# Projections moved between the small compression steps of a fused transformer kernel, and its last expert finished in quarters

## The chip, the cores and the metric

The kernel runs on one core of a Trainium2 chip. The metric is device time in microseconds (us) of one execution. Engines are written as in the profile: PE is TensorE (PEld its weight loads), DVE is VectorE, ACT is ScalarE, POOL is GpSimd, SP is SyncE, which here only issues DMAs. PE's clock has two levels, 1.2 and 2.4 GHz; the profile gives the granted clock as a share of the higher one.

## The reference

A batch of one, 256 tokens, width 1024. Two layers of a first block are followed by one hybrid layer. Everything is float32.

```python
for l in range(2):
    mod = silu(c) @ w_ada[l] + b_ada[l]           # nine shifts, scales, gates
    x = x + 0.5 * g1 * swiglu(modulate(x, sh1, sc1), ...)
    x = x + g2 * token_mix(modulate(x, sh2, sc2), ...)
    x = x + 0.5 * g3 * swiglu(modulate(x, sh3, sc3), ...)
x = rms_norm(x) * final_norm
# hybrid layer: convolution and forgetting attention, then
out = 0
for e in range(32):                               # each token has two experts of one group of 8
    out = out + comb[..., e:e+1] * ((silu(h @ w_gate[e]) * (h @ w_up[e])) @ w_down[e])
return x + gate2 * out
```

The part of `token_mix` that the change reorders:

```python
k_c = gelu(blocks(kc) @ cmpk_w1) @ cmpk_w2        # 15 compressed keys per group; v_c likewise
p_c = masked_softmax(q_a @ k_c.T * scale - slope * d_c); o_c = p_c @ v_c
q = (rms_norm(cq) * mla_q_norm) @ mla_w_uq        # 8 heads x (64 + 32), rope on the last 32
ckv = rms_norm(ckv) * mla_kv_norm
k_nope = ckv @ mla_w_uk;  v = ckv @ mla_w_uv
```

## The kernel before

Each engine has one program, written out by hand, and the engines meet at semaphores. Nothing is scheduled by a tool: the order of the lines in an engine's program is the order of its work.

**Weights.** All weights stream from HBM in units of three blocks of 128 x 2048 floats (1 MB each). SP loads a block into `raw` once the block before it in that place has been split. A split is two halves of 128 x 1024: ACT rounds a half to `w_hi` (L504, for the experts L512), DVE subtracts to get `w_lo` (L933, for the experts L940). ACT may write a place of `w_hi` only when PE has released it (`used[j]`). Every product of an activation with a weight is three matmuls (`mm3`, L1717 to L1719: high by high, high by low, low by high), so 128 x 512 outputs over 128 rows of depth cost three 512-column matmuls.

**The stretch in the token mix** (program of PE from L2016, of DVE from L1319, of ACT from L690). PE turns the latents cq and ckv, q, the selected and window keys, and the keys and values to be compressed (`bank[2]`, `bank[3]`, L2025). Then:

- 16 `keep_warm` matmuls with a matrix of zeros (L1707), while DVE copies the turned rows and builds `blocks` (L1324, L1325, L1331);
- 16 matmuls that compress (L2036), gelu on ACT (L700), 12 small ones that make compressed keys and values (L2044, L2047), 8 more zero matmuls, 16 small score matmuls (L2057);
- q's up-projection: four banks, 36 matmuls of 384 columns; meanwhile DVE and ACT run the softmax of the compressed scores;
- 4 transposes of p (L2073), k's up-projection (12 matmuls of 512), the 16 products with compressed values (L2086), v's up-projection (12 of 512);
- 32 transposes of q and k heads (L1968), and the attention jobs begin: scores of job 0 (L1920), scores of job 1 after DVE has added job 0's bias, and the merge gates' matmuls between jobs (L1717).

DVE applies rope after ACT has copied q's up-projection (L708), copies k's and v's out (L1381, L1396), scales the compressed output (L1390) and copies turned k (L1400). Blocks 1 and 2 of unit `u_mix + 3` are split after all up-projections of q.

```python
                keep_warm(16, SPARE[:, 64:512])
                pe.wait_ge(blocks_ready, l + 1)
                pe.wait_ge(cqT_ready, l * 3 + 3)
                carry_waits()
```

**The experts.** Tokens are gathered into four tiles of 128 by group, and the 32 experts run one after the other on a group's tile: 24 matmuls of gate and up, 12 of down, where expert e's down follows e+1's gate and up. A group's output y stands in `ACC[0]` and `ACC[1]`; `sparse_out` splits it (ACT L880, DVE L1673), and `spread` (L2315) distributes the rows to token order in the four SPREAD banks, summed over the groups. After the last group `x_update` multiplies each SPREAD bank with `gate_bc` into `upd` (L1032) and adds it to x (L1035), token tile by token tile, and SP writes x with one DMA (L464). The last expert's down weights go into place 2 of `w_hi`, which PE releases when expert 30's down is done.

## Time and profile before

| | us |
|---|---|
| median of 3 runs | 1877.88 (1874.67 to 1884.23) |
| the profiled execution's own time | 1885.67 |
| its span in the profile | 1884.0 |
| PE busy | 1785.5 (95%) |
| DVE busy | 1373.1 (73%) |
| ACT busy | 957.4 (51%) |
| POOL busy | 47.0 (2%) |
| mean granted TensorE clock | 0.97 |
| read from HBM | 435.36 MB, 232 GB/s over the span |

Busy shares are means over stages with different limits, and PE counts as busy on zero matmuls and at half clock too. In a timeline row the first number is the start in us from the span's start, the second the length of the merged piece; matmuls overlap, so what one costs is the distance between two starts. A count on PE's rows of float32 products that are not split counts two records for each matmul.

### The profile page before, as it was taken

How to read it: one execution, taken by the hardware profiler on the slowest of the kernel's cores; microseconds unless marked ns; L12 is line 12 of the kernel's file. 1: busy time of each engine (PE TensorE's matmuls, PEld its weight loads, DVE VectorE, ACT ScalarE, POOL GpSimd, SP SyncE). 2: the span in 40 equal slices, each digit the busy share in tenths (PEclk: the TensorE clock that was granted, in tenths of full speed). 3: DMA queues.
4: the chain of work that ended last, by engine and by line, in shares of the span. 5: the costliest groups of instructions: out<-in, count | busy, mean ns of one | idle time of the engine just before them, and what ended most of it. 6: DMA issues, size and time to landing. Idle time of an engine off the chain costs nothing.

```text
span 1884.0 us, 24972 instructions
## 1 busy us (share of the span) xinstructions
PE 1785.5 (95%) x8677; PEld 1443.0 (77%) x8693; DVE 1373.1 (73%) x2091; ACT 957.4 (51%) x1433; POOL 47.0 (2%) x92
## 2 busy tenths in 40 slices
PE   5999999999999999999999999999899897999996
PEld 3788787877788878887878777887787766888875
DVE  6878675856876578777657678776776477998985
ACT  3444453664544454444436554444444546777773
POOL 0000000000000000000000000000000000000000
PEclk8999998999999999999979999999899998999998
DMA  8988651234576658884513348986563433999992
GB/s 366 362 333 302 255 203 63 93 120 170 202 288 245 247 216 322 310 325 174 191 48 110 118 150 298 350 304 231 188 246 108 183 134 138 375 350 363 359 346 98
DMA packets 61499, 437.45 MB, mean 232 GB/s; under 512 B 6768, under 2 KB 7280, under 8 KB 9200
## 3 DMA queue, kind: packets, MB, share of 16 engines
q1 hardware_dynamic: 47200, 339.27, 48.1%
q0 software_dynamic: 12672, 92.28, 13.2%
q10 hardware_dynamic: 1552, 4.89, 0.7%
q8 instruction: 48, 0.79, 0.2%
q14 instruction: 27, 0.22, 0.0%
HBM read 435.36 MB, written 1.05 MB: 232 GB/s over the span
## 4 chain that ended last, share of the span: by engine, by line
PE 83%; DVE 11%; ACT 4%; issue 1%; DMA 1%; ACTq 0%; SPq 0%; DVEq 0%; POOLq 0%
PE bank L1717 24%; PE bank L1718 24%; PE bank L1719 24%; DVE w_lo L933 3%; PE bank L1940 2%; DVE ada_w L957 1%; ACT w_hi L504 1%; PE bank L1958 1%; PE bank L1799 1%; DMA ada_w<-ada_pairs 1%; PE bank L1920 1%; PE bank L1707 1%; DVE arena L1032 1%; DVE w_lo L940 1%; DVE arena L1232 1%
## 5 line engine op out<-in xcount | busy, mean ns | idle before, releaser
L933 DVE TENSOR_TENSOR w_lo<-raw,w_hi 128x1024 fp32r<-128x1024 f32 x426 | 501.5, 1220 | 223.5 <-ACT w_hi L504 222.9
L504 ACT ACTIVATE w_hi<-raw 128x1024 fp32r<-128x1024 f32 x426 | 426.2, 1052 | 363.5 <-PE bank L1719 359.6
L1717 PE MATMUL bank<-w_hi,uT_hi 128*128 128x512 f32 (+3 forms) x1424 | 558.4, 392 | 19.5 <-DVE uT_lo L1251 11.9
L1718 PE MATMUL bank<-w_lo,uT_hi 128*128 128x512 f32 (+3 forms) x1424 | 544.2, 382 | 0.0
L1719 PE MATMUL bank<-w_hi,uT_lo 128*128 128x512 f32 (+3 forms) x1424 | 543.7, 382 | 0.0
L1717 PEld LDWEIGHTS bank<-w_hi,uT_hi 128*128 128x128 f32 x1424 | 271.6, 191 | 78.7 <-DVE uT_lo L1251 12.9
L1719 PEld LDWEIGHTS bank<-w_hi,uT_lo 128*128 128x128 f32 x1424 | 270.9, 190 | 52.1
L1717 PE MATMUL bank<-w_hi,r_arena 128*128 128x512 f32 (+1 forms) x744 | 301.9, 406 | 8.1 <-DVE r_arena L1634 4.9
L1718 PEld LDWEIGHTS bank<-w_lo,uT_hi 128*128 128x128 f32 x1424 | 271.5, 191 | 48.7 <-issue 1.4
L1718 PE MATMUL bank<-w_lo,r_arena 128*128 128x512 f32 (+1 forms) x744 | 298.6, 401 | 0.0
L1719 PE MATMUL bank<-w_hi,r_arena 128*128 128x512 f32 (+1 forms) x744 | 295.7, 397 | 0.0
L957 DVE CUSTOM_DVE_ANT_0 ada_w<-ada_w,cmpw 128x1024 f32<-128x1024 f32 x176 | 206.9, 1218 | 6.3 <-DMA ada_w<-ada_pairs 6.3
L1717 PEld LDWEIGHTS bank<-w_hi,r_arena 128*128 128x128 f32 x744 | 143.0, 192 | 43.7 <-DVE r_arena L1634 5.6
L1719 PEld LDWEIGHTS bank<-w_hi,r_arena 128*128 128x128 f32 x744 | 142.8, 192 | 33.3
L1718 PEld LDWEIGHTS bank<-w_lo,r_arena 128*128 128x128 f32 x744 | 142.9, 192 | 30.6
L940 DVE TENSOR_TENSOR w_lo<-raw,w_hi 128x1024 fp32r<-128x1024 f32 x96 | 113.2, 1221 | 13.1 <-ACT w_hi L512 13.1
L512 ACT ACTIVATE w_hi<-raw 128x1024 fp32r<-128x1024 f32 x96 | 96.2, 1053 | 17.7 <-PE bank L1719 17.7
L554 ACT ACTIVATE arena<-bank 128x256 f32<-128x256 f32 x88 | 33.8, 386 | 121.9 <-PE bank L1719 121.9
L940 DVE TENSOR_TENSOR w_lo<-ada_w,w_hi 128x1024 fp32r<-128x1024 f32 x64 | 75.3, 1221 | 9.7 <-ACT w_hi L512 8.9
L474 POOL DMA_DIRECT2D ada_w<-ada_pairs x88 | 46.8, 531 | 1342.1 <-DVE mods_gate L957 594.6
L512 ACT ACTIVATE w_hi<-ada_w 128x1024 fp32r<-128x1024 f32 x64 | 64.1, 1054 | 13.6 <-PE bank L1719 13.6
L1707 PE MATMUL bank<-zeros 128*128 128x512 bf16 (+1 forms) x236 | 57.7, 399 | 6.3 <-DMA cst<-shape_constants 5.8
(324 smaller groups left out, 1474.8 us busy)
## 6 DMA issues: line engine op xcount, KB each, us to landing
raw<-weight_stream SPq DMA_DIRECT2D x216, 1024.0 KB, 4.9
ada_w<-ada_pairs POOLq DMA_DIRECT2D x88, 1024.0 KB, 5.2
raw<-expert_blocks SPq DMA_DIRECT2D x48, 1024.0 KB, 4.9
ada_w<-expert_blocks SPq DMA_DIRECT2D x32, 1024.0 KB, 4.8
cmpw<-expert_blocks SPq DMA_DIRECT2D x16, 1024.0 KB, 4.9
arena<-ada_pairs SPq DMA_DIRECT2D x5, 1024.0 KB, 13.9
ada_w<-ada_pairs SPq DMA_DIRECT2D x3, 1024.0 KB, 13.3
cmpw<-compress_w ACTq DMA_DIRECT2D x2, 1024.0 KB, 8.1
```

The lines of the kernel that those rows point to most:

```text
L474: pool.dma_start(ada_w[:, slot], ada[g]).then_inc(ada_landed[slot], 16)
L504: act.activation(w_hi[:, b], v, ACT.Copy).then_inc(hi_done, 1)
L512: act.activation(w_hi[:, b], v, ACT.Copy).then_inc(hi_done, 1)
L554: act.activation(act_g[:, t], GU[t][:, 0:F_UNIT], ACT.Silu).then_inc(silu_done, 1)
L933: V.tensor_tensor(w_lo[:, b], v, f32(w_hi[:, b]), ALU.subtract).then_inc(split_done, 1)
L940: V.tensor_tensor(w_lo[:, b], v, f32(w_hi[:, b]), ALU.subtract).then_inc(split_done, 1)
L957: e = V.tensor_tensor_reduce(w[:, i], w[:, i], c, 1.0, 0.0, ALU.mult, ALU.add, dst[:, i:i + 1])
L1707: pe.matmul(dst, zeros[:, 0:P], zeros[:, 0:dst.shape[1]], start=True, stop=True, skip_group_check=True)
L1717: pe.matmul(dst, xh, w_hi[:, off:off + n], start=first, stop=False, skip_group_check=True)
L1718: pe.matmul(dst, xh, w_lo[:, off:off + n], start=False, stop=False, skip_group_check=True)
L1719: return pe.matmul(dst, xl, w_hi[:, off:off + n], start=False, stop=last, skip_group_check=True)
L1940: m = pe.matmul(HT[:, a * DH:(a + 1) * DH], pT[j % 2][:, kt, a], v, start=kt == 0, stop=kt == qt, skip_group_check=True)
```

## The change

Nothing is computed differently, save that the gate of the expert layer multiplies each group's output before it is spread, instead of the sum after.

In the token mix PE's order becomes: q's up-projection right behind the turns of the keys and values to be compressed, in place of the 16 zero matmuls; compression; k's up-projection of token tile 0; the small matmuls of compressed keys and values; k's of tile 1 and v's of tile 0, in place of the 8 zero matmuls; compressed scores; v's of tile 1; transposes of p; q's turns; products with compressed values; k's turns. Banks are dealt out anew for this. DVE builds k's rope part while it has no other work, applies q's rope before compression is done, and takes the copies and splits between.

At the end, the last expert's down weights go to place 0 of `w_hi` (free after its own first four k steps), the down product runs output half by output half, each half is gated (`y_gated`), split, spread, added to x in quarters of 128 x 512, and each quarter has its own DMA.

The core of the diff (not shown: new bank numbers in copies, `first_mod` folded into `mod_ready`, which shifts counts by 3, and the same edits in the branch for a group of over 128 tokens, which this input does not enter):

PE, token mix:

```diff
                 m.then_inc(c_psum, 1)
-                keep_warm(16, SPARE[:, 64:512])
+                pe.wait_ge(q_ready, l * 2 + 2)
+                pe.wait_ge(ks_ready, l + 1)
+                pe.wait_ge(kw_ready, l + 1)
+                seen = set()
+                for b in range(4):
+                    for k in range(3):
+                        off = UQ_OFF + k * 768 + (b % 2) * 384
+                        need(u_mix + 2, seen, off, 384)
+                        m = mm3(bank[UQ_BANKS[b]][:, 0:384], cqT_hi[:, k, tok(b // 2)], cqT_lo[:, k, tok(b // 2)], off, 384, k == 0, k == 2)
+                    m.then_inc(uq_psum, 1)
+                for j in (1, 2):
+                    release(used[j])
...
+
+                def up(t, b, off, done):
+                    for k in range(2):
+                        m = mm3(b[:, :], cqT_hi[:, 3 + k, tok(t)], cqT_lo[:, 3 + k, tok(t)], off + k * 512, 512, k == 0, k == 1)
+                    m.then_inc(done, 1)
+
+                need(u_mix + 3, set(), 0, BLK)
+                up(0, bank[2], 0, uk_psum)
                 pe.wait_ge(hidc_ready, l + 1)
-                pe.wait_ge(q_ready, l * 2 + 2)
+                pe.wait_ge(uq_copied, l * 4 + 4)
                 carry_waits()
...
-
-                keep_warm(8, SPARE[:, 64:512])
+                up(1, bank[3], 0, uk_psum)
+                up(0, bank[0], 1024, uv_psum)
                 pe.wait_ge(kvc_ready, l + 1)
...
+                up(1, bank[1], 1024, uv_psum)
+                release(used[0])
...
+
+                pe.wait_ge(rope_done, l + 1)
+                pe.wait_ge(uk_copied, l * 2 + 2)
+                pe.wait_ge(uv_ready, l * 2 + 2)
+                for b in range(4):
+                    if b == 2:
+                        pe.wait_ge(cp_ready, l + 1)
+                    for i in range(2):
+                        m = turn_rows(bank[Q_BANKS[b]][:, i * S:i * S + S], lambda t, h: q_tok[:, t, h], 2 * b + i, QK)
+                    m.then_inc(qm_psum, 1)
...
                 for b in range(4):
+                    if b < 2:
+                        pe.wait_ge(qm_ready, l * 4 + 3 + b)
+                    else:
+                        pe.wait_ge(co_done, l + 1)
                     for i in range(2):
                         m = turn_rows(bank[K_BANKS[b]][:, i * S:i * S + S], lambda t, h: k_tok[:, t, h], 2 * b + i, QK)
                     m.then_inc(km_psum, 1)
```

ACT and DVE, token mix:

```diff
+                for b in range(4):
+                    act.wait_ge(uq_psum, l * 4 + b + 1)
+                    act.activation(q_tok[:, b // 2, 4 * (b % 2):4 * (b % 2) + 4].rearrange("p h c -> p (h c)"), bank[UQ_BANKS[b]][:, 0:384],
+                                   ACT.Copy).then_inc(uq_copied, 1)
+                split(u_mix + 3, (1,))
                 act.wait_ge(hidc_psum, l + 1)
                 act.activation(hid_cmp[:, :, :, 0:N_CMP], bank[4][:, 0:64].rearrange("p (k g n) -> p k g n", k=2, g=GROUPS)[:, :, :, 0:N_CMP],
                                ACT.Gelu_apprx_tanh).then_inc(hidc_ready, 1)
+                split(u_mix + 3, (2,))
...
+                dve.wait_ge(uq_copied, l * 4 + 4)
+                dve.wait_ge(blocks_ready, l + 1)
+                qr = q_tok[:, :, :, NOPE:QK]
...
+
+                def up_k(t):
+                    dve.wait_ge(uk_psum, l * 2 + t + 1)
+                    V.tensor_copy(k_tok[:, t, :, 0:NOPE], bank[2 + t][:, :].rearrange("p (h c) -> p h c", h=HEADS)).then_inc(uk_copied, 1)
+
+                def up_v(t):
+                    dve.wait_ge(uv_psum, l * 2 + t + 1)
+                    V.tensor_copy(vm[:, t], bank[t][:, :]).then_inc(uv_ready, 1)
+
+                up_k(0)
...
                 e.then_inc(kvc_ready, 1)
-
                 link(V.memset(p_cmp[:, :, :], 0.0))
+                up_k(1)
+                up_v(0)
+                split(u_mix + 3, (2,))
...
+                up_v(1)
```

The expert end (ACT, DVE, PE, SP):

```diff
+                place, sem_, count = expert_place(half, odd, 2, IN_LINE)
+                act.wait_ge(sem_, count)
+                act.wait_ge(used[0], half * 2 + (MOE_U0 + odd + 2))
+                for b, v in halves(0, place):
+                    act.activation(w_hi[:, b], v, ACT.Copy).then_inc(hi_done, 1)
+
...
-                act.wait_ge(ys_psum, n + 1)
                 for h in range(2):
-                    act.activation(y_hi[:, h * 512:(h + 1) * 512], ACC[h][:, :], ACT.Copy).then_inc(ys_hi_done, 1)
+                    act.wait_ge(ys_gated, 2 * n + h + 1)
+                    act.activation(y_hi[:, h * 512:(h + 1) * 512], y_gated[:, h * 512:(h + 1) * 512], ACT.Copy).then_inc(ys_hi_done, 1)
...
+                for h in range(2):
+                    dve.wait_ge(ys_psum, 2 * n + h + 1)
+                    V.tensor_tensor(y_gated[:, h * 512:(h + 1) * 512], ACC[h][:, :], gate_bc[:, h * 512:(h + 1) * 512], ALU.mult).then_inc(ys_gated, 1)
...
+            def last_update(n):
+                for i, (h, t) in enumerate([(h, t) for h in range(2) for t in range(T)]):
+                    dve.wait_ge(spread_done, 4 * n + i + 1)
+                    xt = x[:, t, h * 512:(h + 1) * 512]
+                    V.tensor_tensor(xt, xt, SPREAD[2 * t + h][:, :], ALU.add).then_inc(x_ready, 1)
...
-            x_update(n6 + 1, (spread_done, 1), SPREAD)
+            last_update(0)
...
+                for h in range(2):
+                    for c in range(2):
+                        m = mm3(ACC[h][:, :], hTs_hi[:, c], hTs_lo[:, c], at_ + c * D + h * 512, 512, False, done and c == 1)
+                    if done and h == 0:
+                        m.then_inc(ys_psum, 1)
...
-                        if last and h == 1:
-                            m.then_inc(first_tile if t == 0 else spread_done, 1)
+                        if last:
+                            m.then_inc(spread_done, 1)
...
-            sp.dma_start(out.rearrange("(t p) d -> p t d", p=P), x[:, :, :]).then_inc(out_landed, 16)
+            for i, (h, t) in enumerate([(h, t) for h in range(2) for t in range(T)]):
+                sp.wait_ge(x_ready, 2 * (3 * DEPTH + 3) + i + 1)
+                sp.dma_start(out[t * P:(t + 1) * P, h * 512:(h + 1) * 512], x[:, t, h * 512:(h + 1) * 512]).then_inc(out_landed, 16)
+            sp.wait_ge(out_landed, 64)
```

**On PE, token mix, from the turns of compressed keys on.** L2025 are those turns, L1707 the zero matmuls, L1702 carries waits, L2036 compression, L2044 and L2047 make the compressed keys and values, L2057 scores. Before:

```order
L2025 MATMUL bank<-cst,arena 64x128 x15
L1707 MATMUL bank<-zeros 128x448 x16
L1702 MATMUL bank<-zeros 128x1 [waits cqT_ready,blocks_ready]
L2036 MATMUL bank<-arena,cmpw 128x4x15 x16
L1702 MATMUL bank<-zeros 128x1 [waits q_ready,hidc_ready]
L2044 MATMUL bank<-arena,lvec 64x15 x2
L2047 MATMUL bank<-lvec,arena 15x64 x4
L2044 MATMUL bank<-arena,lvec 64x15 x2
L2047 MATMUL bank<-lvec,arena 15x64 x4
L1707 MATMUL bank<-zeros 128x448 x8
L2057 MATMUL bank<-arena 128x15 [waits kvc_ready]
L2057 MATMUL bank<-arena 128x15 x15
L1717 MATMUL bank<-w_hi,r_arena 128x384 [waits blocks_split,kw_ready,ks_ready]
```

With the change (L1754 to L1756 are `mm3`; the 36 rows of q's up-projection stand above these):

```order
L1735 MATMUL bank<-zeros 128x1 x2
L1739 MATMUL bank<-zeros 128x1 [waits cqT_ready,blocks_ready]
L2084 MATMUL bank<-arena,cmpw 128x4x15 x16
L1754 MATMUL bank<-w_hi,r_arena 128x512 [waits blocks_split]
L1755 MATMUL bank<-w_lo,r_arena 128x512
L1756 MATMUL bank<-w_hi,r_arena 128x512
L1754 MATMUL bank<-w_hi,r_arena 128x512
L1755 MATMUL bank<-w_lo,r_arena 128x512
L1756 MATMUL bank<-w_hi,r_arena 128x512
L1739 MATMUL bank<-zeros 128x1 [waits uq_copied,hidc_ready]
L2100 MATMUL bank<-arena,lvec 64x15 x2
L2103 MATMUL bank<-lvec,arena 15x64 x4
```

The zero matmuls are gone, q's 36 matmuls fill the time in which DVE builds the blocks, and six matmuls of k's stand between compression and what needs its gelu.

**On ACT, token mix.** L695 and L697 copy q, L698 and L700 the selected keys. Before, the two activation functions stand first, then q's up-projection is copied out (L708), then p (L711), then both splits (L504):

```order
L698 ACTIVATE arena<-bank 128x512 [waits ks_psum]
L700 ACT_TABLE_LOAD
L700 ACTIVATE arena<-bank 128x4x15 [waits hidc_psum]
L704 ACT_TABLE_LOAD
L704 ACTIVATE arena<-arena 128x16x15 [waits cs_ready]
L708 ACTIVATE arena<-bank 128x384 [waits uq_psum] x4
L711 ACTIVATE arena<-bank 128x512 [waits cp_psum]
L504 ACTIVATE w_hi<-raw 128x1024 [waits block_used1,block_landed1]
L504 ACTIVATE w_hi<-raw 128x1024
L504 ACTIVATE w_hi<-raw 128x1024 [waits block_used2,block_landed2]
L504 ACTIVATE w_hi<-raw 128x1024
L715 ACTIVATE cmpw<-bank 96x512 [waits qm_psum] x4
```

With the change:

```order
L700 ACTIVATE arena<-bank 128x512 [waits ks_psum]
L703 ACTIVATE arena<-bank 128x384 [waits uq_psum] x4
L506 ACTIVATE w_hi<-raw 128x1024 [waits block_used1,block_landed1]
L506 ACTIVATE w_hi<-raw 128x1024
L707 ACT_TABLE_LOAD
L707 ACTIVATE arena<-bank 128x4x15 [waits hidc_psum]
L506 ACTIVATE w_hi<-raw 128x1024 [waits block_used2,block_landed2]
L506 ACTIVATE w_hi<-raw 128x1024
L712 ACT_TABLE_LOAD
L712 ACTIVATE arena<-arena 128x16x15 [waits cs_ready]
L714 ACTIVATE arena<-bank 128x512 [waits cp_psum]
L717 ACTIVATE cmpw<-bank 96x512 [waits qm_psum] x4
```

The copies of q's up-projection and one split now stand ahead of the gelu and its table load, the other split ahead of the exponential and its table load.

**On DVE, the expert end.** From the last expert's hidden product (L1646) on, before:

```order
L1646 SCALAR_TENSOR_TENSOR arena<-arena,bank 128x256 [waits silu_done]
L940 TENSOR_TENSOR w_lo<-raw,w_hi 128x1024 [waits blocks_hi] x2
L1634 TENSOR_TENSOR r_arena<-bank,r_arena 128x256 [waits hT_hi_done]
L1673 TENSOR_TENSOR y_split<-bank,y_split 128x512 [waits ys_hi_done] x2
L1032 TENSOR_TENSOR arena<-bank,gate_bc 128x512 [waits first_tile,gate_ready]
L1032 TENSOR_TENSOR arena<-bank,gate_bc 128x512
L1035 TENSOR_TENSOR x<-x,arena 128x1024 [waits vector_chain]
L1032 TENSOR_TENSOR arena<-bank,gate_bc 128x512 [waits spread_done]
L1032 TENSOR_TENSOR arena<-bank,gate_bc 128x512
L1035 TENSOR_TENSOR x<-x,arena 128x1024 [waits vector_chain]
```

With the change:

```order
L1670 SCALAR_TENSOR_TENSOR arena<-arena,bank 128x256 [waits silu_done]
L1658 TENSOR_TENSOR w_lo<-raw,w_hi 128x1024 [waits blocks_hi] x2
L1652 TENSOR_TENSOR r_arena<-bank,r_arena 128x256 [waits hT_hi_done]
L1701 TENSOR_TENSOR arena<-bank,gate_bc 128x512 [waits ys_psum] x2
L1704 TENSOR_TENSOR y_split<-arena,y_split 128x512 [waits ys_hi_done] x2
L1711 TENSOR_TENSOR x<-x,bank 128x512 [waits spread_done] x4
```

Four products with the gate and two additions of 1024 columns became two products (ahead of the split) and four additions of 512 columns, each behind its own signal from PE.

## Rows read from the trace of the kernel before

**Rows 1.** The page: span, busy time by engine, and the chain that ended last.
```profile
span 1884.0 us, 24972 instructions
PE 1785.5 (95%) x8677; PEld 1443.0 (77%) x8693; DVE 1373.1 (73%) x2091; ACT 957.4 (51%) x1433; POOL 47.0 (2%) x92
...
PE 83%; DVE 11%; ACT 4%; issue 1%; DMA 1%; ACTq 0%; SPq 0%; DVEq 0%; POOLq 0%
```

**Rows 2.** Windows: us from start, engines' busy us, then granted TensorE clock, DMA.
```profile
293.50:336.60 43.10, 39.13 (x257) 31.52 (x253) 24.90 (x63) 10.31 (x16) 0.00 (x0) 0.84 0.16 53
933.00:980.90 47.90, 43.88 (x257) 36.13 (x253) 24.90 (x63) 10.31 (x16) 0.00 (x0) 0.75 0.14 49
301.40:308.20 6.80, 6.49 (x44) 3.74 (x43) 2.40 (x11) 1.50 (x2) 0.00 (x0) 0.50 0.00 0
939.70:960.20 20.50, 20.19 (x102) 17.40 (x101) 5.56 (x25) 2.40 (x4) 0.00 (x0) 0.50 0.00 1
```

**Rows 3.** Timeline, TensorE, layer 0: start, us, engine, line, operation, count, [idle before].
```profile
293.56 3.20 PE L1707 MATMUL bank<-zeros 128*128 128x448 bf16 x16
298.47 4.39 PE L2036 MATMUL bank<-arena,cmpw 128*128 128x60 f32 x32
...
307.72 3.55 PE L2057 MATMUL bank<-arena 64*128 64x15 f32 x32
...
319.66 0.48 PE L1717 MATMUL bank<-w_hi,r_arena 128*128 128x512 f32 x1
...
322.64 2.60 PE L2086 MATMUL bank<-arena 15*128 15x64 f32 x32
...
329.67 3.24 PE L1968 MATMUL bank<-cst,arena 128*96 128x128 f32 x28
...
336.67 1.14 PE L1920 MATMUL bank<-arena 64*128 64x256 f32 x8 [1.52 <-DVE arena L1181]
```

**Rows 4.** Timeline, ScalarE and VectorE, layer 0.
```profile
303.14 1.28 ACT L704 ACT_TABLE_LOAD   x1
...
325.62 1.67 DVE L1390 TENSOR_TENSOR arena<-bank,arena 128x128 f32<-128x128 f32 x8
...
332.70 2.47 DVE L1400 COPY cmpw<-bank 96x512 f32<-96x512 f32 x4
```

**Rows 5.** Timeline, TensorE, layer 1.
```profile
937.97 5.49 PE L2036 MATMUL bank<-arena,cmpw 128*128 128x60 f32 x32
...
948.32 6.18 PE L2057 MATMUL bank<-arena 64*128 64x15 f32 x32
...
980.92 1.14 PE L1920 MATMUL bank<-arena 64*128 64x256 f32 x8 [1.52 <-DVE arena L1181]
```

**Rows 6.** Timeline, expert end, all engines but weight loads.
```profile
1859.17 0.48 DVE L1646 SCALAR_TENSOR_TENSOR arena<-arena,bank 128x256 f32<-128x256 f32 x1 [2.53 <-ACT arena L872]
...
1861.48 2.00 ACT L512 ACTIVATE w_hi<-raw 128x1024 fp32r<-128x1024 f32 x2 [2.42 <-PE bank L1719]
1862.57 2.36 DVE L940 TENSOR_TENSOR w_lo<-raw,w_hi 128x1024 fp32r<-128x1024 f32 x2 [2.91 <-ACT w_hi L512]
...
1865.31 0.80 PE L1717 MATMUL bank<-w_hi,r_arena 128*128 128x512 f32 x1 [3.71 <-DVE r_arena L1634]
...
1870.17 0.63 PE L1719 MATMUL bank<-w_hi,r_arena 128*128 128x512 f32 x1
...
...
1879.04 0.40 SPq L464 DMA_DIRECT2D out<-x  x1
```

**Rows 7.** DMA issues: line, engine, count, KB each, median us to landing.
```profile
out<-x SPq DMA_DIRECT2D x1, 1024.0 KB, 4.6
arena<-final_norm_rows ACTq DMA_DIRECT2D x1, 512.0 KB, 3.4
```

**Rows 8.** Timeline, second expert group's start.
```profile
1661.15 1.28 DVE L1673 TENSOR_TENSOR y_split<-bank,y_split 128x512 fp32r<-128x512 f32 x2
...
1663.31 2.02 PE L2315 MATMUL bank<-y_split,picks 128*128 128x512 f32 x8
```

158 lines of the change are left out of this document (58 added, 100 removed).

## The prediction

> **What bounds the kernel.** The page comes first [rows 1]: PE is busy for 95% of the span, and the chain that ended last lies on it for 83%. A change saves time where it takes work off PE, closes a gap of PE, lets PE run at its full clock, or shortens what comes after PE's last product. So the second view is the windows over the two stretches that are reordered, one in each layer, each taken from the first zero matmul to the scores of attention job 1 [rows 2]. They take 43.1 and 47.9 us. PE is busy in over 90% of both, yet the granted clock averages 0.84 and 0.75: busy and slow. From 301.4 to 308.2 in layer 0, and from 939.7 to 960.2 in layer 1, it is 0.50, which is the 1.2 GHz level. The third view is PE's timeline, which gives each piece its price, and DVE's beside it [rows 3, 4, 5]. The last one is the timeline of the expert end [rows 6], where nothing runs beside the chain ACT, DVE, PE, DVE, SP.
>
> **Prices.** Split matmuls of 512 columns cost 0.24 us at full clock (12 from 319.66 to the row at 322.64, with the start of the first, make 0.25 each) [rows 3], and 0.44 at half (11 steps from 1865.31 to 1870.17) [rows 6]. Those of 384 columns are taken at three quarters, 0.18 and 0.33. Compression costs 4.4, the compressed scores 3.5 at full clock and 6.2 at half [rows 3, 5], the products with compressed values 2.6, a turn 0.116 (28 records, one each, in 3.24) [rows 3]. The 12 small matmuls of compressed keys and values have no row of their own here: between compression's end at 302.9 and the scores at 307.72 stand they, 0.3 of waiting, and 8 zero matmuls at half clock, twice 0.20 each [rows 2, 3]; 1.3 is left.
>
> **The token mix, at full clock.** Added up from the first of q's matmuls:
> - q's up-projection, 36 x 0.18: 6.5. It starts where the zero matmuls did (293.56), since all it needs was copied before. It hides what the 16 zero matmuls and the gap behind them covered, 4.9 us until compression at 298.47, so blocks are ready when PE comes.
> - Compression 4.4; k of tile 0 1.4 (6 x 0.24), which hides the gelu. On ACT, four copies and one split (2.0, as in rows 6) now stand ahead of the gelu and its table load. The last copy can end about 0.6 after q's product, so split (2.0) and load (1.3) [rows 4, 6] end within the 4.4 of compression. I cost them at nothing; without that cover PE would wait for the gelu.
> - 12 small ones 1.3; k of tile 1 and v of tile 0 2.9, against DVE's copies of compressed keys and values, which they about cover.
> - Scores 3.5; v of tile 1 1.4; then PE waits for the exponential, which needs DVE and ACT in turn. DVE is late here, as it has taken two copies and a split before: estimate 0.8.
> - 4 transposes of p 0.5; 16 turns of q 1.9; compressed values 2.6.
> - From there DVE decides: 8 products 1.7, 4 copies of k 2.5 [rows 4], then job 0's bias, 1.5 until PE's scores of job 1, as now [rows 3], and 0.4 of signals: 6.1. PE's own turns and scores fit in that. This is a new wait: now the products' copies lie beside v's up-projection.
>
> The sum is 33.3 per layer, thus 9.8 saved in layer 0 and 14.6 in layer 1: **24.4 at full clock**. The DMA queues lose nothing: blocks 1 and 2 of unit u_mix + 3 are split some 20 us earlier, so SP's next loads start earlier in a time when DMA moves 53 GB/s [rows 2].
>
> **The clock.** Not all of it will run at 2.4 GHz. The clock fell 2.9 us after compression began in layer 0 and 1.7 after in layer 1, with PE busy in both [rows 2, 3, 5]: narrow matmuls do not hold it. In layer 0 it rose again behind the 8 zero matmuls; in layer 1 it did not, and all of the scores (6.2) and most of q's up-projection ran at half [rows 2, 5]. With the change wide matmuls stand behind every narrow group, but only 1.4 to 2.9 us of them. I expect a fall in compression that costs the 12 wide ones behind it 0.2 each, 2.4; one in the scores that costs the next 6 another 1.1; and one in the compressed values, mostly under DVE's wait, 0.7. That is 4.2 per layer. The bounds are 0 and about 9 (as large a share of half clock as layer 1 shows now); I take the lower half, because q's 36 matmuls ahead are dense and the longest half-clock stretch, layer 1's, was fed by a gap and narrow work in a row. The mix then gains 24.4 - 8.4 = **16.0** (6 to 24).
>
> The Trainium skill, TensorE: Matmul & The Clock Gate, section "Why this matters for your kernels", puts drops down to idle gaps between bursts of matmuls, and asks to keep PE fed. By this rule the clock would hold wherever PE is fed, and the mix would gain the whole 24.4 (the first rival, below); the trace disagrees, with 0.50 granted while PE was busy for 20.19 of 20.50 us.
>
> **The expert end.** The last down weights no longer wait for expert 30's down. ACT can split them once the last silu is out, at about 1859.1, where DVE's hidden product starts [rows 6], and not at 1861.48. The split ends on DVE 3.45 after its start on ACT (1861.48 to 1864.93), so at 1862.5, with 0.4 for hidden's low part at 1862.9: PE starts 2.4 earlier. Its gap of 3.71 shrinks to 1.3, so I expect the 12 matmuls at full clock: 2.9 and not 5.3, 2.4 saved. From the end of down to the last addition it is 8.4 now (1870.6 to 1879.04). With the change: gating the second half 0.65, low parts of both 1.3 (two in 1.28) [rows 8], four additions of 512 at the same 0.65, 0.1 of signal, 4.7 in all: 3.7 saved, with spread hidden under them. The output DMA ends 5.0 after its issue; a quarter is 256 KB, and from 4.6 for 1024 KB and 3.4 for 512 KB [rows 7] I estimate 2.8 to 3.0 behind the last addition (bounds 2.2 and 4.6): 2.0 saved. Together **10.5** (7 to 11.5; the low end has down at half clock again).
>
> **The other group ends.** At three of them DVE has two operations more, 1.3 us, and ACT waits for DVE before it rounds y. DVE's low parts end at 1662.4, PE spreads at 1663.31 [rows 8]; with the change the halves are ready at about 1663.1 and 1663.7, and PE wants the second 0.9 after the first. Costed at 0.5 in all (0 to 3.9, all of DVE's time). The merged semaphores cost nothing; they add no wait.
>
> **Sum.** 16.0 + 10.5 - 0.5 = 26.0 us less. The profiled execution took 1885.67 and would take 1859.7; it lies 7.8 above the median of the runs. Against the median, 1877.9 - 26.0 = **1852 us**.
>
> **The rivals.**
> - The clock holds. For it: q's dense matmuls replace a gap, and no narrow group is behind another. Against it: compression alone is 4.4 us of narrow work, and the clock fell inside it both times. Gain 24.4 + 10.5 - 0.5 = 34.4: 1843.5. Chance 0.13.
> - The clock takes the mix back. For it: layer 1 today, and the zero matmuls are gone that brought the clock back in layer 0. Extra 8 per layer: the mix gains 8.4, the whole 18.4: 1859.5. Chance 0.23.
> - DVE becomes the bound. It now carries the copies, both splits and rope between compression and scores, and the k copies before job 0; if PE waits 3 us more for it in each layer, and 1 at each group end, 26 - 6 - 3 = 17: 1861. Chance 0.05.
> - The zero matmuls were what kept the clock for the attention jobs. If PE enters them at half clock and stays there, their 192 gate matmuls in a layer cost 0.2 each, 38 us. Then one such layer gives 1852 + 38 = 1890, slower than now; it decides from about 130 wide matmuls at half clock (26 / 0.2). Against it: today the clock comes back behind at most 7 us of dense matmuls, and these are dense. Chance 0.02.
> - The change does less than it says: the order is as written, but PE already waits for something else in that stretch, such as the landing of a block for ACT's early split. SP issued it before the stretch, so little speaks for it. Gain of the end alone, 10: 1868. Chance 0.03.
> - The forecast: 0.54.
>
> **The numbers.** A measurement of this kernel can tell about 0.5%, 9.4 us, from no change. All cases but the slower one are beyond it with their middles; only the ends of the weak ones reach into it. Faster 0.95, same 0.03, slower 0.02. The range of 8 in 10 runs from a little below the first rival to above the second and third: 1841 to 1865.
>
> **What would show it.** In the profile after: q's matmuls of 384 columns start behind the turns with no gap and cost 0.18; compression follows 6.5 later; job 1's scores come 36 to 39 us after the first of them in both layers, with a wait for DVE of about 2 before; the granted clock in the two stretches is above 0.84 and 0.75; the last down starts within 1.5 of the last turn of hidden; and four output DMAs are issued about 0.65 apart, the last some 3 us before the end. Wrong would be: half clock for over 15 us in a layer, PE waiting for a low part of weights (L952) or for y in the groups, or a last DMA that ends over 4.5 us after its issue.

## The result and the profile after

The changed kernel takes 1855.78 us in the median of 5 runs (1848.40 to 1861.46), the kernel before 1877.88. The ratio is 0.9875, with a 95% interval of 0.9852 to 0.9899: 19 to 28 us less, where 26 were forecast, and 1855.8 where the text said 1852. It is faster by more than 0.5%, and the time lies in the range.

The page of the profiled execution (its own time 1855.78, span 1854.1), with the share of each engine in the chain that ended last:

```profile
span 1854.1 us, 24899 instructions
PE 1764.3 (95%) x8645; PEld 1427.1 (77%) x8645; DVE 1376.3 (74%) x2097; ACT 957.9 (52%) x1433; POOL 46.9 (3%) x92
...
PE 82%; DVE 11%; ACT 4%; issue 2%; DMA 1%; ACTq 0%; SPq 0%; DVEq 0%; POOLq 0%
```

Against [rows 1] PE lost 21 us of busy time and kept its share. PE still bounds the kernel.

The windows over the two reordered stretches of the changed kernel, from the first of q's matmuls to the scores of job 1, then over the time at half clock in each (columns as in [rows 2]: us, busy time of PE, PEld, DVE, ACT, POOL, granted clock, DMA share, GB/s):

```profile
296.78:331.00 34.22, 31.72 (x232) 27.61 (x230) 25.17 (x64) 11.69 (x17) 0.00 (x0) 0.90 0.21 72
925.87:959.08 33.21, 30.48 (x232) 26.32 (x230) 25.30 (x64) 11.59 (x17) 0.00 (x0) 0.91 0.20 74
314.70:321.50 6.80, 6.80 (x27) 5.53 (x27) 4.15 (x12) 1.12 (x3) 0.00 (x0) 0.50 0.47 154
953.00:963.20 10.20, 8.08 (x29) 5.58 (x30) 7.69 (x17) 2.89 (x9) 0.00 (x0) 0.50 0.00 0
```

43.1 and 47.9 us became 34.2 and 33.2, and the mean clock in them rose from 0.84 and 0.75 to 0.90 and 0.91. In layer 1, 20.5 us at half clock shrank to 10.2, of which 6.1 lie ahead of job 1's scores.

TensorE's timeline in layer 0 of the changed kernel (start, us, engine, line, operation, count, idle before):

```profile
296.78 0.45 PE L1754 MATMUL bank<-w_hi,r_arena 128*128 128x384 f32 x1
...
303.33 3.76 PE L2084 MATMUL bank<-arena,cmpw 128*128 128x60 f32 x32
306.90 0.47 PE L1754 MATMUL bank<-w_hi,r_arena 128*128 128x512 f32 x1
...
308.40 0.18 PE L1739 MATMUL bank<-zeros 128*128 128x1 bf16 x1
...
312.41 4.15 PE L2113 MATMUL bank<-arena 64*128 64x15 f32 x32
316.48 0.79 PE L1754 MATMUL bank<-w_hi,r_arena 128*128 128x512 f32 x1
317.08 0.63 PE L1755 MATMUL bank<-w_lo,r_arena 128*128 128x512 f32 x1
...
327.16 1.08 PE L2005 MATMUL bank<-cst,arena 128*96 128x128 f32 x8 [0.81 <-DVE arena L1413]
328.17 1.14 PE L1957 MATMUL bank<-arena 64*128 64x256 f32 x8
331.00 1.14 PE L1957 MATMUL bank<-arena 64*128 64x256 f32 x8 [1.69 <-DVE arena L1192]
```

q's product starts without a gap and lasts 6.55 us; compression follows at once; k's first six matmuls (306.90 to 308.40) cover the gelu whole, since the row behind them has no idle time. The clock falls at 314.7, inside the compressed scores; v's six matmuls behind them run at 0.43 us each instead of 0.23. Two waits are left, both for DVE: 0.81 for the products with compressed values, 1.69 for job 0's bias. In layer 1 the scores ran at full clock (3.32 us), and the clock fell only at 953.0, in that wait of 0.81.

The expert end of the changed kernel, all engines but weight loads:

```profile
1838.37 2.00 ACT L873 ACTIVATE w_hi<-raw 128x1024 fp32r<-128x1024 f32 x2
...
1839.45 2.36 DVE L1658 TENSOR_TENSOR w_lo<-raw,w_hi 128x1024 fp32r<-128x1024 f32 x2 [0.39 <-ACT w_hi L873]
...
1840.63 0.38 PE L2327 MATMUL bank<-cst,arena 128*128 128x128 f32 x2
...
1842.20 0.50 PE L1754 MATMUL bank<-w_hi,r_arena 128*128 128x512 f32 x1 [1.19 <-DVE r_arena L1652]
...
1845.11 0.18 PE L2341 MATMUL bank<-zeros 128*128 128x1 bf16 x1
...
1846.68 2.11 PE L2353 MATMUL bank<-y_split,picks 128*128 128x512 f32 x8 [1.40 <-DVE y_split L1704]
1847.45 2.48 DVE L1711 TENSOR_TENSOR x<-x,bank 128x512 f32<-128x512 f32 x4
1848.17 2.12 SPq L466 DMA_DIRECT2D out<-x  x4
```

The low part of the last weights ends at 1841.81, and hidden's low part follows on DVE; PE's gap is 1.19 and not 3.71 [rows 6]; down takes 2.91 at full clock and not 5.3; the last quarter is issued at 1849.96, 4.85 behind the end of down, where it was 8.4. From that last issue to the end are 4.1 us, where one DMA took 5.0.

**Where the 29.9 us between the two traces lie.** I cut both at the same places: the start of the turns of compressed keys, the scores of job 1, the last turn of hidden.

| part | before | changed | difference |
|---|---|---|---|
| start to layer 0's turns | 291.65 | 294.88 | +3.2 |
| layer 0, turns to job 1's scores | 45.02 | 36.12 | -8.9 |
| to layer 1's turns | 594.48 | 592.97 | -1.5 |
| layer 1, turns to job 1's scores | 49.77 | 35.11 | -14.7 |
| to the last turn of hidden | 880.30 | 881.55 | +1.3 |
| last turn to the end | 22.78 | 13.47 | -9.3 |

The parts where nothing but the experts' gate was changed differ by 1 to 3 us either way, and their half clock with them (13.7 us of it ahead of the first turns before, 20.5 after). The changed parts sum to 32.9 us, yet the medians lie only 22.1 apart. That gap was the first thing to explain.

### The profile page after: what moved, and what is told of

Its sections match the earlier page's. It is cut to its first block, busy times and chain, and to the rows that moved or that the text cites. A ratio compares the mean times of both kernels' runs of the same rounds, so it can differ in the third digit from the quotient of the medians.

```text
span 1854.1 us, 24899 instructions
## 1 busy us (share of the span) xinstructions
PE 1764.3 (95%) x8645; PEld 1427.1 (77%) x8645; DVE 1376.3 (74%) x2097; ACT 957.9 (52%) x1433; POOL 46.9 (3%) x92
## 4 chain that ended last, share of the span: by engine, by line
PE 82%; DVE 11%; ACT 4%; issue 2%; DMA 1%; ACTq 0%; SPq 0%; DVEq 0%; POOLq 0%
PE bank L1754 24%; PE bank L1755 24%; PE bank L1756 24%; DVE w_lo L945 2%; PE bank L1977 2%; DVE ada_w L969 1%; ACT w_hi L506 1%; PE bank L1995 1%; DMA ada_w<-ada_pairs 1%; PE bank L1836 1%; PE bank L1957 1%; DVE arena L1243 1%; PE bank L2005 1%; PE bank L1955 1%; PE bank L2297 1%
## 5 line engine op out<-in xcount | busy, mean ns | idle before, releaser
L1754 PE MATMUL bank<-w_hi,uT_hi 128*128 128x512 f32 (+3 forms) x1424 | 558.4, 392 | 20.3 <-DVE uT_lo L1260 12.6
L1756 PE MATMUL bank<-w_hi,uT_lo 128*128 128x512 f32 (+3 forms) x1424 | 543.4, 382 | 0.0
L1754 PEld LDWEIGHTS bank<-w_hi,uT_hi 128*128 128x128 f32 x1424 | 271.5, 191 | 80.1 <-DVE uT_lo L1260 14.0
L1756 PEld LDWEIGHTS bank<-w_hi,uT_lo 128*128 128x128 f32 x1424 | 270.7, 190 | 52.1
L1754 PE MATMUL bank<-w_hi,r_arena 128*128 128x512 f32 (+1 forms) x744 | 299.1, 402 | 6.2 <-DVE r_arena L1652 2.3
L1756 PE MATMUL bank<-w_hi,r_arena 128*128 128x512 f32 (+1 forms) x744 | 292.6, 393 | 0.0
L1754 PEld LDWEIGHTS bank<-w_hi,r_arena 128*128 128x128 f32 x744 | 140.8, 189 | 42.0 <-DVE r_arena L1652 3.0
L1756 PEld LDWEIGHTS bank<-w_hi,r_arena 128*128 128x128 f32 x744 | 140.4, 189 | 32.9
L614 ACT ACTIVATE arena<-arena,stat 128x256 f32<-128x256 f32 (+1 forms) x112 | 49.4, 444 | 23.6 <-DVE stat L1195 23.5
```

What stands on the lines that cost most here:

```text
L614: e = act.activation(v, v, ACT.Exp, bias=nmax[j % 2][:, h:h + 1], accum_out=psum_row[j % 4][:, h:h + 1])
L1754: pe.matmul(dst, xh, w_hi[:, off:off + n], start=first, stop=False, skip_group_check=True)
L1756: return pe.matmul(dst, xl, w_hi[:, off:off + n], start=False, stop=last, skip_group_check=True)
```

## The experiments

Eleven more programs ran, one of them the kernel before once more, in three batches beside fresh runs of the kernel before, whose medians there were 1878.6 to 1879.1. "Stretch" is from the turns of compressed keys to job 1's scores, in layers 0 and 1; "end" from the last turn of hidden. A single trace of a stretch scatters by several us, as will be seen. The second trace of before and the runs on the last split, on one output DMA and on doubled scores are one execution each, so they are read by their traces alone; the others have 4 to 10.

### Each half of the change alone, and before a second time

Mix only: before, with the edits of the token mix (ACT, DVE, PE, banks). End only: before, with all the others. Their cores:

```diff
-                keep_warm(16, SPARE[:, 64:512])
...
+                for b in range(4):
+                    for k in range(3):
+                        off = UQ_OFF + k * 768 + (b % 2) * 384
+                        need(u_mix + 2, seen, off, 384)
+                        m = mm3(bank[UQ_BANKS[b]][:, 0:384], cqT_hi[:, k, tok(b // 2)], cqT_lo[:, k, tok(b // 2)], off, 384, k == 0, k == 2)
+                    m.then_inc(uq_psum, 1)
```

```diff
-                expert_split(half, odd, (2,), IN_LINE if last else LAST_BEHIND)
+                if last:
+                    last_split(half, odd)
```

> The change's token mix with the expert end of before. Theory A (the trace pair is typical): the two stretches, from the first matmul behind the turned compressed keys to the scores of attention job 1, take about 34.2 and 33.2 us and together save 23.6 us, so the time is near 1877.9 - 23.6 = 1854. Theory B (before's one profiled execution had bad luck with the clock in layer 1; the two medians lie only 22.1 apart, and the expert end took 9.3 of that in the trace pair): the mix gains 22.1 - 9.3 = 12.8 against a typical execution, 1865. The expert end takes 22.8 from the last turn of hidden to the end, as before. Rival: the mix order lowers the clock in the attention jobs behind it; then the part between the stretches (596.4 us before) grows by over 2.

> The change's expert end with the token mix of before. From the last turn of hidden to the end 13.5 us in place of 22.8: 9.3 saved, near 1868.6, if the parts add up. The gates at the other three group ends cost nothing that shows (0.05 between the first turned output and the next expert in the trace pair). If the parts do not add up, because the clock after the mix is what made the last down product run at full speed, down takes 5.3 again and the gain is about 7, near 1871.

> The kernel before, unchanged, for a second trace. Theory A: the stretches take 43 and 48 us again, with some 20 us at half clock in layer 1. Theory B: layer 1 takes about 43 like layer 0, with the half clock of a shorter part. Everything up to the first stretch differs from the first trace only where the granted clock does.

Measured: mix only 1862.15, ratio 0.9911 (0.9892 to 0.9931), 17 us less. End only 1873.83, ratio 0.9966 (0.9945 to 0.9987), 6.4 us less (2 to 10). The two sum to 23, the whole change gives 23.5 by its ratio: the halves add up. The end alone was expected at 9.3 and its own trace shows 8.1 to 9.2 less than the old ends below; by its runs it is the smaller 6.4, within an interval that just reaches 10. The windows over the stretches of three traces of the old order, in this order: before, its second trace, end only.

```profile
291.65:336.67 45.02, 40.97 (x285) 33.24 (x285) 25.87 (x66) 11.81 (x18) 0.00 (x0) 0.85 0.19 66
931.15:980.92 49.77, 45.73 (x285) 37.86 (x285) 25.85 (x66) 11.81 (x18) 0.00 (x0) 0.76 0.16 59
```

```profile
294.17:340.82 46.65, 42.60 (x286) 35.06 (x286) 25.87 (x66) 11.81 (x18) 0.00 (x0) 0.82 0.18 64
936.90:981.24 44.34, 39.78 (x285) 33.26 (x285) 25.86 (x66) 11.81 (x18) 0.00 (x0) 0.88 0.18 68
```

```profile
292.42:333.68 41.26, 36.69 (x286) 30.72 (x286) 25.88 (x66) 11.81 (x18) 0.00 (x0) 0.96 0.19 70
927.33:968.58 41.25, 36.68 (x285) 30.71 (x285) 25.87 (x66) 11.80 (x18) 0.00 (x0) 0.96 0.19 71
```

The same program takes 41.3 to 49.8 us for the same work, and the whole spread is in PE's busy time and the granted clock. At 0.96 both layers take 41.25. Theory B is right: layer 1 of the first trace was the worst of six, though the mix gains more than the 12.8 that this theory drew from it. The mean of the old order is 44.3 and 45.1. The new order, in the four traces that have it unchanged (changed kernel, mix only, and the two runs on the expert end below), took 36.12, 36.17, 36.12 and 34.52 in layer 0 and 35.11, 36.64, 35.29 and 36.75 in layer 1: mean 35.7 and 35.95. So the mix is worth **17.7 us** in the mean of these traces, 16.7 by the runs of mix only. With three old traces whose two stretches sum to 94.8, 91.0 and 82.5, the first of these figures is good to a few us only.

The part between the stretches took 594.5, 596.1 and 593.7 us in the old order and 593.0, 596.1, 593.0 and 597.7 in the new: nothing is given back in the attention jobs.

Where the clock falls differs too. In the old order compression stands behind a gap of 1.68 us, and in these six layers the clock fell inside it three times (0.7, 1.7 and 2.9 us after its start) and held three times. In the nine traces of this document that have q's product in front of compression (in one of them the zero matmuls as well) and no gap, it held through all 18.

The end is 22.78, 21.69 and 21.90 where it is old (before twice, mix only), and 13.47 and 13.54 where it is new: 8.6 us. Of the traces with the old end, the first one's whole last down product ran at half clock behind the gap of 3.7, in the others its first six matmuls did and the clock came back within it.

### The zero matmuls, taken out of the old order

```diff
-                keep_warm(16, SPARE[:, 64:512])
...
-                keep_warm(8, SPARE[:, 64:512])
```

> The kernel before without its 24 zero matmuls in each token mix; everything else stays, PE waits where they were. If the zero matmuls only fill waits and do nothing for the clock, the time is within 2 us of before. If they bring the clock back, the stretches hold more half clock: up to 8 us longer each, 1894 at most. If they feed its fall by nothing and cost PE time themselves (the 8 before the scores, where PE waits for DVE's copies), the stretches are 0 to 1 us shorter each.

Measured: 1887.80, ratio 1.0045 (1.0027 to 1.0064), 8.5 us slower than before. TensorE's timeline in layer 0, and the windows over the stretches:

```profile
298.14 0.18 PE L1702 MATMUL bank<-zeros 128*128 128x1 bf16 x1 [4.81 <-DVE arena L1331]
298.18 6.99 PE L2035 MATMUL bank<-arena,cmpw 128*128 128x60 f32 x32
...
309.14 6.17 PE L2055 MATMUL bank<-arena 64*128 64x15 f32 x32 [2.14 <-DVE arena L1338]
```

```profile
291.37:340.73 49.36, 40.05 (x261) 36.04 (x261) 25.86 (x66) 11.81 (x18) 0.00 (x0) 0.76 0.16 59
936.77:984.52 47.75, 38.43 (x262) 34.77 (x262) 25.88 (x66) 11.81 (x18) 0.00 (x0) 0.79 0.17 62
```

The scores' row of before stood at 3.55 and 6.18 [rows 3, 5]. Behind a gap of 4.81 us compression runs at half clock from its start in both layers (6.99, and 7.06 in layer 1, against 3.76 at full), and so do the scores (6.17 against 3.3). The stretches are 97.1 us together, 7.7 above the mean of the old order. The zero matmuls cost PE nothing, since it waited there anyway, and they earned some 8 us of clock: the two stretches hold 44.4 us at half clock here, 23.9 in the mean of the old order.

### The zero matmuls, put back into the new order

```diff
                 for j in (1, 2):
                     release(used[j])
+                keep_warm(16, SPARE[:, 64:512])
                 pe.wait_ge(blocks_ready, l + 1)
...
                 up(0, bank[0], 1024, uv_psum)
+                keep_warm(8, SPARE[:, 64:512])
                 pe.wait_ge(kvc_ready, l + 1)
```

> The changed kernel with the 24 zero matmuls of each token mix put back: 16 between q's up-projection and compression, 8 between v's first up-projection and the compressed scores. From the first turn of compressed keys to the scores of job 1 the changed kernel took 36.1 and 35.1 us. Theory A (the zero matmuls helped the old order because they filled waits; with dense work in those waits they are only work): 3.2 + 1.6 us more per layer at full clock, up to 9.6 in all, less what they give back, so 5 to 10 us slower than the changed kernel, about 1863. Theory B (narrow compression and scores need them even now, and half clock costs the changed kernel more than they do): the half clock of 6 to 7 us per stretch goes, and the time is within 3 us of the changed kernel.

Measured: 1863.40, ratio 0.9921 (0.9903 to 0.9938), 8.6 us over the changed kernel by the two ratios. The stretches:

```profile
290.61:330.35 39.74, 38.12 (x285) 31.62 (x285) 26.20 (x66) 11.90 (x18) 0.00 (x0) 0.91 0.22 80
924.84:964.22 39.38, 36.64 (x286) 30.31 (x286) 26.29 (x66) 11.79 (x18) 0.00 (x0) 0.96 0.21 79
```

They are 4.0 and 3.4 above the means of the new order. The zeros themselves are 3.03 and 1.62 us at full clock, 4.65 a layer, so they give back only about 1 in clock. Theory A holds: the same 24 instructions that saved 8 us in the old order cost 7 to 9 in the new one, because real work stands where PE used to wait.

### q's product early, but k's and v's not woven in

```diff
-                need(u_mix + 3, set(), 0, BLK)
-                up(0, bank[2], 0, uk_psum)
                 pe.wait_ge(hidc_ready, l + 1)
...
-                up(1, bank[3], 0, uk_psum)
-                up(0, bank[0], 1024, uv_psum)
                 pe.wait_ge(kvc_ready, l + 1)
...
+                need(u_mix + 3, set(), 0, BLK)
+                up(0, bank[2], 0, uk_psum)
+                up(1, bank[3], 0, uk_psum)
+                up(0, bank[0], 1024, uv_psum)
                 up(1, bank[1], 1024, uv_psum)
...
-                up_k(0)
                 dve.wait_ge(kvc_psum, l + 1)
...
-                up_k(1)
-                up_v(0)
...
+                up_k(0)
+                up_k(1)
+                up_v(0)
                 up_v(1)
```

> The changed kernel with k's and v's up-projections taken out of the weave: q's 36 matmuls first, then compression, compressed keys and values and their scores in a row, then all 24 matmuls of k and v, and DVE's four copies of them behind the softmax's maximum. Nothing is left out. If the weave matters as cover, PE waits for the gelu (about 1.5) and for DVE's copies of compressed keys and values (about 2.5) in each layer; if it matters for the clock too, compression to scores runs at half clock and costs another 3 to 6. So 4 us longer per stretch by cover alone, 7 to 10 with the clock; in all 8 to 20 over the changed kernel. If q's early place alone does it all, the stretches stay within 1 us of 36.

Measured: 1865.21, ratio 0.9938 (0.9920 to 0.9956), 11.8 us over the changed kernel. TensorE in layer 0, then the windows:

```profile
299.91 3.76 PE L2084 MATMUL bank<-arena,cmpw 128*128 128x60 f32 x32
303.98 0.18 PE L1739 MATMUL bank<-zeros 128*128 128x1 bf16 x1 [0.31 <-ACT arena L707]
...
307.20 6.17 PE L2109 MATMUL bank<-arena 64*128 64x15 f32 x32 [2.13 <-DVE arena L1374]
```

```profile
291.46:332.83 41.37, 36.07 (x261) 31.97 (x262) 26.29 (x66) 11.80 (x18) 0.00 (x0) 0.83 0.21 76
927.41:969.74 42.33, 37.18 (x261) 32.76 (x261) 26.46 (x66) 11.91 (x18) 0.00 (x0) 0.80 0.19 72
```

The stretches are 5.6 and 6.4 over the means of the new order. Cover makes up about 2.8 of it in each layer (waits of 0.31 for the gelu, 2.13 for DVE's copies of compressed keys and values, and 0.36 for its copy of v ahead of q's turns). The other 3 to 4 I put down to the clock: 13.7 and 17.1 us of the stretches are at half clock, where the new order has 3.4 to 10.2; with wide matmuls between them the scores took 3.3 to 4.15, here 6.17. Of the mix's 17.7 us, q's early place with the zeros gone gives 5.7 (89.4 to 83.7) and the weave 12. My expectation of 4 for cover alone was too high: the table load ran while PE was compressing (302.41 to 303.69), so the gelu cost 0.31 and not 1.5.

### Narrow matmuls without a gap

Each of the 16 compressed score matmuls is issued twice in a row.

```diff
                         for i in range(4):
-                            m = pe.matmul(bank[4 + p][:, 64 * qt + 16 * i:64 * qt + 16 * i + N_CMP], qT[half, i, tok(qt)], kT_cmp[half, i // 2, 0:N_CMP],
-                                          start=True, stop=True, skip_group_check=True)
+                            for _ in range(2):
+                                m = pe.matmul(bank[4 + p][:, 64 * qt + 16 * i:64 * qt + 16 * i + N_CMP], qT[half, i, tok(qt)], kT_cmp[half, i // 2, 0:N_CMP],
+                                              start=True, stop=True, skip_group_check=True)
```

> The changed kernel with each of the 16 compressed score matmuls issued twice in a row. The stretch has no gap of PE ahead of them, so this tells narrow matmuls from gaps. If narrow work lets the clock fall, the second half of the scores and v's last up-projection run at half clock in both layers (6.2 for each 16 at that clock, 0.43 us for each of the six wide ones), so the stretch is 5 to 7 us longer, with 7 to 14 us at half clock. If only gaps do, the added scores cost 3.3 and the half clock stays at 6 to 7 us or falls.

Measured in one execution: 1861.30. Layer 0 and the windows (the stretches, then the scores ahead of the fall and behind it):

```profile
307.64 11.01 PE L2114 MATMUL bank<-arena 64*128 64x15 f32 x64
318.58 0.79 PE L1754 MATMUL bank<-w_hi,r_arena 128*128 128x512 f32 x1
319.18 0.63 PE L1755 MATMUL bank<-w_lo,r_arena 128*128 128x512 f32 x1
```

```profile
290.12:333.04 42.92, 40.42 (x293) 36.17 (x293) 26.10 (x66) 11.85 (x18) 0.00 (x0) 0.84 0.20 73
925.99:967.98 41.99, 40.35 (x294) 35.59 (x294) 26.27 (x66) 12.13 (x18) 0.00 (x0) 0.84 0.20 74
307.60:309.90 2.30, 2.30 (x21) 2.26 (x21) 2.30 (x4) 0.00 (x0) 0.00 (x0) 0.99 0.21 89
309.90:318.60 8.70, 8.70 (x47) 8.66 (x46) 1.14 (x2) 0.00 (x0) 0.00 (x0) 0.50 0.34 121
```

PE has no gap ahead of the fall or behind it; it is busy for all of the 11.0 us. The clock falls 2.3 us after the scores begin; in layer 1, again with no gap, 4.6 us after. The stretches are 7.2 and 6.0 longer, with 13.7 us at half clock in each. In both layers the clock fell during narrow matmuls in a row, with PE busy all the time; and the run without zeros shows that it falls at a gap too.

### The expert end, piece by piece

The last down weights split late, into place 2, the rest of the new end kept:

```diff
-                if last:
-                    last_split(half, odd)
-                else:
+                if not last:
                     expert_split(*after(half, odd), (1,))
-                    expert_split(half, odd, (2,))
+                expert_split(half, odd, (2,), IN_LINE if last else LAST_BEHIND)
...
-                    sparse_down(u + PER_GROUP - 1, f + PER_GROUP - 1, IN_LINE, done=True, clear=n == EXPERT_GROUPS, at_=0)
+                    sparse_down(u + PER_GROUP - 1, f + PER_GROUP - 1, IN_LINE, done=True, clear=n == EXPERT_GROUPS)
```

> The changed kernel with the last down weights split into place 2 again, behind expert 30's down, everything else of the new end kept. PE's gap before the last down product grows from 1.2 to about 3.6. If that gap is what lowers the clock, down's 12 matmuls take 5.3 and not 2.9, and the end takes 13.5 + 2.4 + 2.4 = 18.3 from the last turn of hidden; if the fall in before came by chance, 15.9.

One output DMA behind the last addition:

```diff
-            for i, (h, t) in enumerate([(h, t) for h in range(2) for t in range(T)]):
-                sp.wait_ge(x_ready, 2 * (3 * DEPTH + 3) + i + 1)
-                sp.dma_start(out[t * P:(t + 1) * P, h * 512:(h + 1) * 512], x[:, t, h * 512:(h + 1) * 512]).then_inc(out_landed, 16)
...
+            sp.wait_ge(x_ready, 2 * (3 * DEPTH + 3) + 4)
+            sp.dma_start(out.rearrange("(t p) d -> p t d", p=P), x[:, :, :]).then_inc(out_landed, 16)
...
```

> The changed kernel with one output DMA of 1 MB behind the last addition, in place of four of 256 KB. From the end of the last addition to the end it took 5.0 in the kernel before and about 4.1 now. Forecast of step 1: the quarters save 2.0. By the trace pair they save 0.8, so the end should take 14.3 in place of 13.5.

Late split, the last down product and what follows:

```profile
1841.39 0.80 PE L1750 MATMUL bank<-w_hi,r_arena 128*128 128x512 f32 x1 [3.72 <-DVE r_arena L1650]
1841.99 0.63 PE L1751 MATMUL bank<-w_lo,r_arena 128*128 128x512 f32 x1
...
1846.68 0.23 PE L2337 MATMUL bank<-zeros 128*128 128x1 bf16 x1
```

The gap is 3.72 again, all 12 matmuls run at half clock (5.29 us), and the end takes 18.50 where 18.3 was expected. The early split is worth 5.0 us in this pair, half of it the gap and half the clock that goes with it; where the clock comes back after six matmuls (down then takes 4.2) it is 1.1 less. With one DMA the end takes 14.45: the four DMAs are worth 0.95. What is left of the 8.6, gating ahead of spread and adding in quarters, is therefore 2.7 to 3.8; no run isolated it, and the trace pair shows 3.6 between the end of down and the last addition.

### Two attempts at a better version

Both let ACT copy k's turned rows instead of DVE; one sends the output in two DMAs of 512 KB, the other sends the quarters in turn from SP and ACT.

```diff
+                for b in range(4):
+                    act.wait_ge(km_psum, l * 4 + b + 1)
+                    act.activation(qkT_m[0:QK, 1, 2 * b:2 * b + 2], bank[K_BANKS[b]][0:QK, :].rearrange("p (h s) -> p h s", h=2),
+                                   ACT.Copy).then_inc(km_ready, 1)
...
-                for b in range(4):
-                    turned_k(b)
```

```diff
+            for h in range(2):
+                act.wait_ge(x_ready, 2 * (3 * DEPTH + 3) + 2 * h + 2)
+                act.dma_start(out[P:S, h * 512:(h + 1) * 512], x[:, 1, h * 512:(h + 1) * 512]).then_inc(out_landed, 16)
```

> The changed kernel with two edits at different places: ACT copies k's turned rows in place of DVE in the token mix, and the output goes in two DMAs of 512 KB, each behind two additions. Token mix: DVE reaches job 0's bias 2.5 us earlier and then waits for PE's scores; I expect the wait of PE before job 1's scores to end 0.8 to 1.2 us earlier in each layer, if ACT is not late with the copies. Output: from the last addition to the end 4.1 with quarters, 5.1 with one DMA. If the 2 KB rows of the quarters make their last packets late, two DMAs still have them (3.9 to 4.3); if it is the number of DMAs, 3.4.

> The changed kernel with k's turned rows copied by ACT as in the run two_out_dmas, and the four output DMAs issued in turn by SP and by ACT, whose engine is idle there. If each queue's last packets are what comes late, the end comes 0.3 to 0.8 earlier than with SP alone (3.3 to 3.8 behind the last issue); if all 16 DMA engines are full until 3 us behind it, nothing changes (4.1).

Measured: 1851.90 (0.9862, 0.9834 to 0.9890) and 1853.45 (0.9879, 0.9851 to 0.9907); neither can be told from the changed kernel. TensorE and VectorE in layer 0 of the first:

```profile
323.36 1.14 PE L1955 MATMUL bank<-arena 64*128 64x256 f32 x8
324.64 1.42 DVE L1196 SCALAR_TENSOR_TENSOR arena<-cst,bank 128x256 f32<-128x256 f32 x4 [2.34 <-PE bank L1955]
326.08 1.22 DVE L1199 TENSOR_REDUCE stat<-arena 128x4 f32<-128x1024 f32 x1
326.11 1.14 PE L1955 MATMUL bank<-arena 64*128 64x256 f32 x8 [1.60 <-DVE arena L1196]
```

A miss. DVE now sits idle for 2.34 us and job 1's scores come 2.75 behind job 0's, against 2.83 with the copies on DVE. The copies had lain beside PE's turns and scores all along. The end took 13.41 and 13.49 in these two, 13.47 with four DMAs from SP: two DMAs or four, one queue or two, made no difference once the first half left early.

## Why the prediction was right, step by step

- **Sum and sign.** The forecast was 26.0 less, the ratio of runs gives 23.5 and the parts measured over several traces 26.3 (17.7 and 8.6). The terms:

| term | forecast | measured |
|---|---|---|
| token mix | 16.0 | 17.7 in the mean of the traces, 16.7 by the runs of mix only |
| expert end | 10.5 | 8.6 in the mean of the traces, 9.3 in the trace pair, 6.4 (2 to 10) by the runs of end only |
| group ends | -0.5 | within 0.1 |

- **The mix came out right by two errors that cancel.** Counted from the first of q's matmuls, I gave the new stretch 33.3 at full clock and 4.2 for the clock, 37.5. It takes 33.9 in the mean (35.8 less 1.9 of turns). And I subtracted it from one trace in which the old order took 43.1 and 47.9, where its mean is 42.4 and 43.2. Each new stretch is 3.6 shorter than the text said, 7.2 in all, and the two old ones together are 5.4 shorter than their first trace. That the two errors are of like size is luck; the order of the work and what it hides were forecast rightly.
- **Which prices were too high.** Compression was read at 4.4 from a row in which the clock had fallen [rows 3]; at full clock it is 3.6 from start to next start. The 12 small matmuls are 1.0, not 1.3. The scores are 3.3, not 3.5, and the wait for the exponential is 0 to 0.39, not 0.8. From the products with compressed values to job 1's scores, "DVE decides: 6.1", is 5.7, and the copies of k are no part of it, as the attempt with ACT showed: what decides is PE's wait for the products (0.81) and for the bias. Together these make 1.7 a layer: layer 1 of the changed kernel, with its last pieces, at half clock, put at what layer 0 shows for them (5.7 in place of 7.4), takes 31.6 and not 33.3. The other 1.9 is the clock's term, sized at 4.2 and by this 2.3 in the mean (33.9 less 31.6).
- **The clock.** That it would fall in spite of the dense work was right. Of the three places named, the scores took it in layer 0 and the time behind the compressed values in layer 1. In compression, where I expected the first fall because the one trace had it in both layers, it held in all 18 layers traced with q's product early. I put that down to q's dense matmuls in front; that the gap of 1.68 us is gone fits as well, and no run separates the two. The rival "the clock holds" was wrong: the changed kernel has 6.8 and 6.1 us of half clock, and the mix gives 17.7 and not 24.4.
- **Cover.** Gelu, table load and copies behind k's and v's matmuls: costed at nothing, seen at nothing. Take the cover away and it is 2.8 us of waiting in each layer, 0.31 of it for the gelu, and as much again in clock.
- **The expert end.** Early split: 2.4 of gap and 2.4 of clock forecast, 5.0 measured, though 3.9 where the clock comes back early. From down's end to the last addition 3.7 forecast, 3.6 in the trace pair. The term that failed is the output DMA, "2.0 saved": it is 0.95. I took a quarter's own 2.8 to 3.0 us from issue to landing as what follows the last addition, and set it against 5.0 from issue to the end. But the end comes 0.4 behind the landing, with one DMA (4.6 and 5.0) as with four (3.7 and 4.1). And the quarters' median is 2.6, but the last one takes longest:

```profile
DMA to landing us min/median/max: 2.4/2.6/3.7
```

The additions come 0.6 us apart, so the four transfers overlap, and the last one lands 3.7 behind its issue. That it shares the DMA engines with the others I argue from this; the two queues, which changed nothing, speak for it, but no run isolated it.
- **Group ends.** From the first gate matmul of the next expert to the one behind spread are 7.74, 7.74 and 7.79 us at the three group ends, against 7.69, 7.68 and 7.80 before. The two added products per group are hidden.
- **The rivals.** "The clock takes the mix back" is refuted for the new order, and the run without zero matmuls shows how it would have looked: 47.8 to 49.4 us a stretch. The slower one, half clock carried into the attention jobs, did not happen in any trace; behind job 1's scores at most 4.2 us were at half clock (layer 1 of the changed kernel, to 963.2). That PE waits for DVE 3 us more was refuted too: 0.81 and 1.69 against 0.53 and 1.52 before.

The standing of the one profiled execution was read rightly (7.8 above its median), but I did not ask which part of it was slow. It was the stretch on which the forecast stood.

Of the signs that were named, most came: no gap ahead of q's matmuls, compression 6.5 later, four DMAs 0.6 apart, a last down 1.19 behind the last turn. Two were missed, both with the errors above: job 1's scores came 34.2 and 33.2 us after the first of q's matmuls and not 36 to 39, and the last DMA was issued 4.1 ahead of the end and not 3.

## What to carry to other kernels

Zero matmuls are free only where PE would wait anyway. In this kernel's waits of 4.8 and 2.1 us they saved some 8 us; once real wide matmuls stood in those places, which did about as much for the clock, the same zeros cost 7 to 9. Between groups of narrow matmuls put wide ones, in pieces as long as the next group's inputs take to be ready; here the weave was worth twice as much as the move alone. And before a forecast rests on a stretch with half clock in it, take a second trace: the same program took 41 to 50 us for it.
